# Two dense attentions: the next head's high halves on GpSimd, and the inverse sums moved out of PSUM by ScalarE

## What is computed

```python
def dense_gqa_attention(q, k, v):            # attention A: 8 heads of 64, 2 key heads
    sc = jnp.einsum('bqkgd,bskd->bkgqs', qi, k).astype(jnp.float32) * scale
    p = jax.nn.softmax(sc, axis=-1).astype(v.dtype)
    return jnp.einsum('bkgqs,bskd->bqkgd', p, v)
...
def even_mixer(...):
    oa = dense_gqa_attention(qa, ka, va) * jax.nn.silu(ga)
    ...
    # attention B: scores are a part of 64 (q_nope against keys) plus a rotary part of 32
    ob = mla_attention(q_lat, q_rope, ckv, k_rope, w_uv) * jax.nn.silu(gb)
    return jnp.concatenate([oa, ob], axis=-1) @ w_out
```

## Time and profile before

| | before |
|---|---|
| median of 3 runs | 2436.44 us (2435.43 to 2438.64) |
| the profiled execution: time, span of its core | 2435.96 us, 2434.6 us |
| TensorE busy | 2342.3 us, 96% of the span |
| VectorE, ScalarE, GpSimd busy | 1399.0, 1139.0, 893.7 us |
| shares of the chain of work that ended last | PE 80%, ACT 7%, issue 5%, DVE 4%, POOL 2% |
| attention A | about 294 to 490 us of the span |
| attention B | about 529 to 755 us of the span |

### The profile page before, as it was taken

How to read it: one execution, slowest core, us unless ns; L and a number is a source line. 1 busy time by engine, 2 the same in 40 slices (tenths; PEclk the granted TensorE clock), 3 DMA queues, 4 the chain that set the end, 5 groups by cost and what they waited for, 6 DMA issues and landing times.

```text
span 2434.6 us, 31485 instructions
## 1 busy us (share of the span) xinstructions
PE 2342.3 (96%) x12138; PEld 1936.1 (80%) x12138; DVE 1399.0 (57%) x1931; ACT 1139.0 (47%) x1778; POOL 893.7 (37%) x665
## 2 busy tenths in 40 slices
PE   5999999989999999998999999999999999999998
PEld 5778788868888888876678878788877888888887
DVE  6256499948885240129973744332576666666665
ACT  5322388868884231239962375232333333333334
POOL 1111234236662122326522212112255555565551
PEclk8999999999999999999999999999999999999999
DMA  8244300000003131100021131113111111111111
GB/s 304 75 130 139 103 6 1 1 19 1 1 1 113 35 125 44 52 9 1 10 104 44 45 116 44 29 32 121 52 44 52 52 52 52 52 52 53 57 55 70
DMA packets 152488, 143.23 MB, mean 59 GB/s; under 512 B 10358, under 2 KB 140692, under 8 KB 150420
## 3 DMA queue, kind: packets, MB, share of 16 engines
q1 hardware_dynamic: 152340, 141.22, 18.1%
HBM read 124.43 MB, written 16.78 MB: 58 GB/s over the span
## 4 chain that ended last, share of the span: by engine, by line
PE 80%; ACT 7%; issue 5%; DVE 4%; POOL 2%; DMA 0%; SPq 0%; ACTq 0%; DVEq 0%; POOLq 0%
PE ps L260 38%; PE ps L2617 15%; PE ps L2634 9%; PE ps L1103 4%; PE ps L1126 3%; PE ps L1113 3%; ACT C_PR L1773 1%; PE ps L1662 1%; POOL WSL L2534 1%; ACT B_PR L1186 1%; ACT B_PTH L1180 1%; PE ps L2593 1%; ACT C_PTH L1781 1%; PE ps L1641 1%; POOL WSR L2516 1%
## 5 line engine op out<-in xcount | busy, mean ns | idle before, releaser
L249 POOL TENSOR_TENSOR WL<-WR,WH 128x1024 fp32r<-128x1024 f32 (+1 forms) x89 | 206.3, 2318 | 805.8 <-ACT WH L244 805.6
L260 PE MATMUL ps<-HH,WH 128*128 128x512 f32 (+1 forms) x1136 | 359.8, 398 | 0.0
L260 PE MATMUL ps<-HL,WH 128*128 128x512 f32 (+1 forms) x1136 | 351.4, 391 | 0.0
L260 PE MATMUL ps<-HH,WL 128*128 128x512 f32 (+1 forms) x1136 | 351.1, 390 | 0.0
L260 PEld LDWEIGHTS ps<-HH,WL 128*128 128x128 f32 (+1 forms) x1136 | 212.7, 187 | 46.5
L260 PEld LDWEIGHTS ps<-HL,WH 128*128 128x128 f32 (+1 forms) x1136 | 212.5, 187 | 46.7
L260 PEld LDWEIGHTS ps<-HH,WH 128*128 128x128 f32 (+1 forms) x1136 | 209.1, 187 | 48.1 <-issue 6.3
L2847 DVE TENSOR_TENSOR XF<-ps,XF 128x1024 f32<-128x1024 f32 x168 | 201.6, 1220 | 32.4 <-PE ps L2634 25.8
L2617 PE MATMUL ps<-HC,WSH 128*128 128x512 f32 x640 | 197.0, 389 | 0.0
L1139 DVE TENSOR_REDUCE NM<-ps 128x1 f32<-128x1024 f32 x128 | 156.1, 1220 | 34.9 <-PE ps L1103 34.2
L2534 POOL TENSOR_TENSOR WSL<-WSR,WSH 128x512 fp32r<-128x512 f32 x100 | 131.4, 1314 | 107.5 <-ACT WSH L2528 107.5
(11 more groups left out here) (433 smaller groups left out, 5179.1 us busy)
## 6 DMA issues: line engine op xcount, KB each, us to landing
WS<-in_w_ffn_in SPq DMA_DIRECT2D x44, 512.0 KB, 4.9
MKW<-in_ada_w SPq DMA_DIRECT2D x32, 512.0 KB, 4.1
spill<-X SPq DMA_DIRECT2D x3, 4096.0 KB, 13.5
OW<-in_w_ffn_out SPq DMA_DIRECT2D x22, 512.0 KB, 3.4
WR<-in_w_in SPq DMA_DIRECT2D x20, 512.0 KB, 3.7
WR<-in_odd_w_in SPq DMA_DIRECT2D x19, 512.0 KB, 3.7
WR<-in_even_w_in SPq DMA_DIRECT2D x17, 512.0 KB, 4.9
AWK<-in_ada_w SPq DMA_DIRECT2D x8, 1024.0 KB, 9.6
```

Of the source, the lines that this page charges most:

```text
L249: pool.tensor_tensor(low[:, :, :], raw[:, :, :], high[:, :, :].bitcast(F32), ALU.subtract).then_inc(*w_low.up(t))
L260: last = pe.matmul(ps[0:w.m, 2 * s + h, :], wt[:, k, :], x[:, k, halves(h)], start=(k == 0 and n == 0), stop=(k == w.kt - 1 and n == 2))
```

## The change

Four things change, in both attentions:

1. The high halves of the next head's queries (two pieces for each of heads 1 to 7) move from ScalarE to GpSimd: `pool_query`, in GpSimd's step s % 8 = 1. ScalarE keeps the keys' and rotary highs of B, now in steps 3, 4 and 5 in place of 3, 4 and 4.
2. GpSimd's low pieces move one step later (2 to 6 in place of 1 to 5), its values from step 5 to step 7.
3. The product of the gate and the inverse sums moves from VectorE, which read the inverse sums in PSUM, to GpSimd. Since that reads a tile in SBUF, ScalarE first copies the inverse sums to a new tile `RIS` (64 x 256). There is one such tile for each attention, so ScalarE waits for GpSimd's product of the pair before.
4. GpSimd begins attention A only when the last projection of the stage before has been multiplied.

```diff
-    gated = signal("gated")
+    ri_moved = signal("ri_moved")
...
-    mixed, ri_wide, v_high, v_low, bias_low, *pool_lows = pool_made.steps("mixed", "ri_wide", "v_high", "v_low", "bias_low",
-                                                                          "q_low", "k_low", "r_low")
+    mixed, ri_wide, v_high, v_low, pool_gated, pool_q_high, *pool_lows = pool_made.steps(
+        "mixed", "ri_wide", "v_high", "v_low", "gated", "q_high", "q_low", "k_low", "r_low")
...
-    A.RID = place("A_RID", 187.5, [P, 2, HD])
+    A.RID, A.RIS = place("A_RID", 187.5, [P, 2, HD]), place("A_RIS", 43, [P, 2 * P])
...
-    B.RID = place("B_RID", 203.5, [P, 2, HD])
+    B.RID, B.RIS = place("B_RID", 203.5, [P, 2, HD]), place("B_RIS", 67, [P, 2 * P])
...
         if piece < 2:
-            if h >= 2 and piece == 0:
-                act.wait_ge(*s_done.at(g, 8 * (h - 2) + 7))
             act.activation(D.QD1[h % 2][rows(piece, HD), :], D.q(h), ACT.Copy).then_inc(*q_high.up(g, h, piece))
...
+    def pool_query(D, h, piece):
+
+        g = D.tag
+        if h >= 2 and piece == 0:
+            pool.wait_ge(*s_done.at(g, 8 * (h - 2) + 7))
+        pool.tensor_copy(D.QD1[h % 2][rows(piece, HD), :], D.q(h)).then_inc(*pool_q_high.up(g, h, piece))
+
...
-            eng.wait_ge(*q_high.at(g, h, 1))
+            eng.wait_ge(*(pool_q_high if h else q_high).at(g, h, 1))
...
-                mix = MIX[o, D.mix(h), rows(pg % 4, 2 * P)]
-                dve.wait_ge(*pv_done.at(g, pg))
-                dve.tensor_tensor(mix, ps[0:HD, 6 + pg % 2, 2 * P:4 * P], mix, ALU.mult).then_inc(*gated.up(g, pg))
...
                 act.wait_ge(*pv_done.at(g, pg))
+                if pg:
+                    act.wait_ge(*pool_gated.at(g, pg - 1))
+                act.activation(D.RIS[rows(pg // 4 % 2, HD), :], ps[0:HD, 6 + pg % 2, 2 * P:4 * P],
...
                 if pg >= 2:
                     act.wait_ge(*o2_done.at(g, pg - 2))
                 act.activation(D.OT[rows(pg // 4 % 2, HD), pg % 2, :], ps[HD:P, 6 + pg % 2, 0:2 * P],
...
             h = s // 8 + 1
             if h < 8:
-                for piece in {1: (0, 1), 3: (2,), 4: (3, 4)}.get(s % 8, ()):
-                    if piece < 2 or g == "B":
+                for piece in {3: (2,), 4: (3,), 5: (4,)}.get(s % 8, ()):
+                    if g == "B":
                         act_query(D, h, piece)
...
-                pool.wait_ge(*gated.at(g, pg))
+                pool.wait_ge(*ri_moved.at(g, pg))
+                pool_in_turn()
+                pool.tensor_tensor(mix, D.RIS[o, :], mix, ALU.mult).then_inc(*pool_gated.up(g, pg))
                 pool.wait_ge(*o2_done.at(g, pg))
                 pool_in_turn()
...
             h = s // 8 + 1
             if h < 8:
-                for piece in {1: (0,), 2: (1,), 3: (2,), 4: (3,), 5: (4,)}.get(s % 8, ()):
+                if s % 8 == 1:
+                    for piece in range(2):
+                        pool_in_turn()
+                        pool_query(D, h, piece)
+                for piece in {2: (0,), 3: (1,), 4: (2,), 5: (3,), 6: (4,)}.get(s % 8, ()):
                     if piece < 2 or g == "B":
                         pool_in_turn()
                         rest_query(pool, D, h, piece)
-                if s % 8 == 5 and D.v_first(h):
+                if s % 8 == 7 and D.v_first(h):
...
     def pool_attention_a():
         pool.wait_ge(*va_copied.at())
+        pool.wait_ge(*w_used.at(EVEN_PROJ[-1]))
```

More of the change, by code:

```diff
@@ L1190, in act_dense @@
                 act.wait_ge(*pv_done.at(g, pg))
+                if pg:
+                    act.wait_ge(*pool_gated.at(g, pg - 1))
+                act.activation(D.RIS[rows(pg // 4 % 2, HD), :], ps[0:HD, 6 + pg % 2, 2 * P:4 * P],
+                               ACT.Copy).then_inc(*ri_moved.up(g, pg))
                 if pg >= 2:
```

## The result

The changed kernel takes 2447.47 us (median of 5 runs, 2444.62 to 2449.24), the kernel before beside it 2436.44 (2434.47 to 2438.64). The ratio is 1.0041, 95% interval 1.0028 to 1.0054: slower by 11.0 us. The forecast was 2437.7, its range ended at 2446. In two later jobs the changed kernel took 2445.37 and 2445.51, which is 8.5 and 7.5 us more than the kernel before.

A forecast was written before the change was run, and what follows sets the result against it. TensorE was taken to set the pace in both attentions. A -8.6, B +8.2 (stalls 17.1 less gains 8.9) and clock +1.7 sum to +1.3 us: 2437.7 us against the median 2436.44, range 2431 to 2446.

The forecast's parts named there:

- I leave the clock at 1.00 in the stalls of 2.2 us: In B, clock loss of 1.7 us was counted only behind head 3's 5.0 us stall, none behind the shorter ones.
- the clock falls in every stall: Rival for B: five more clock falls of 1.7 us each, 2446.2 us in all; chance 0.13.
- A, step 6 to 63, -7.0: Attention A's 8.3 us excess from ScalarE's query highs goes, except 1.3 us for weight pieces: -7.0 us.
- A's start, -1.6: At A's start, ScalarE's two query copies no longer stand before the first PTH: 1.6 us gained.
- ScalarE's highs in B, -7.6: In B, moving query highs away and splitting the two rotary highs of step 4 removes all 7.6 us excess.
- The cast of 64x1024 at 1.04 us: GpSimd's new query cast, absent from the trace, takes 1.04 us by a line through smaller copies and casts.
- rival of a dearer copy: GpSimd's query cast takes 1.54 us, giving 2443.7 us, or 2.39 us, giving 2454; chance 0.10.
- The chain of 21.3 us: GpSimd's work in B from a head's first RID to its last rotary low: 19.3 us busy plus 2.0 us gaps.
- Stalls of 2.2 us each: In B, TensorE waits 2.2 us for GpSimd's last low at heads 2, 4, 5, 6 and 7: 11.0 us.
- Head 3, 5.0: In B, head 3's stall is 5.0 us, since its GpSimd chain also holds EVEN_FIRST's low and starts later.
- Head 1, 1.1: In B, head 1 waits 1.1 us: its first RID comes late and the second rotary high is made later.
- A late product in A: GpSimd's product in A, 1.2 us late, stays hidden; rival: it stops ScalarE, 8.4 us more, 2446.1 us, chance 0.07.

The follow-up runs named there:

- e1: The changed kernel run again with nothing altered: 2445.37 us, ratio 1.0032 to the kernel before.
- e11: The changed kernel again, unaltered, on the same chip as the run with shorter TensorE filler products: 2445.51 us, ratio 1.0034 to the kernel before.
- e8: Changed kernel, but B's gate product on VectorE, B's lows, values and highs not later, EVEN_FIRST's low in step 22: 2424.33 us, 0.9947 of the kernel before.
- e4: Changed kernel, but B's gate product back on VectorE and ScalarE's RIS copy gone there: 2429.09 us, 0.9968 of the kernel before.
- e6: A as changed; B as before except later steps for GpSimd's lows and values and ScalarE's second rotary high: 2432.21 us, 0.9976 of the kernel before.
- e3: Change in attention B alone, A as in the kernel before: 2455.06 us, ratio 1.0079 to the kernel before.
- e5: Changed kernel plus unused identity products on TensorE before B's waits for lows (16 a head, 34 in head 3): 2452.14 us, 1.0062 of the kernel before.
- e9: Changed kernel plus unused identity products on TensorE before B's waits for lows (8 a head, 17 in head 3): 2438.90 us, 1.0009 of the kernel before.

## Why the prediction was wrong

**The failing step** is the sentence "I leave the clock at 1.00 in the stalls of 2.2 us". It counted one fall, 1.7 us, where the profiles of after lost 5.1, 8.5 and 8.5 us to the clock in B, which made B's steps 4.2, 7.3 and 7.2 us longer. The one fall that it did count was sized too low as well: behind head 3's stall the steps were 2.4 to 2.6 us longer. The rival *the clock falls in every stall* was the right mechanism with too high a count: two to four of the six stalls of 1.8 us or more, in the three profiles of after. Its 2446.2 is nearer to the three medians (2445.4 to 2447.5) than the forecast is, and the range ended 0.2 us short of it. By the runs, the mean result is -8.1 in A, +9.1 from stalls in B (224.0 against 214.9) and +7.0 from the clock by the steps of e1 and e11: +8.0, against 8.5 and 7.5 measured there. The forecast had -8.6, +8.2 and +1.7.

The other steps:

- **A, step 6 to 63, -7.0:** measured -6.55. The weight pieces of steps 16 to 20 kept 1.7 us, not 1.3.
- **A's start, -1.6:** -1.5. **B's start, -1.3:** from 16.8 to 15.5 us, -1.3.
- **ScalarE's highs in B, -7.6:** e8 shows 191.37 us from step 6 to step 63, of 189.8 at the clean pace and 197.45 before. So 6.1 of the 7.6 came there, in a kernel whose highs stand in other steps (its start, 16.6 us, gained only 0.2). In the changed kernel the gain can't be read apart from the stalls.
- **The cast of 64x1024 at 1.04 us:** 1037 ns. The line through copies and casts held. The rival of a dearer copy is out. The estimate of 1.54 us from the price in the Trainium skill (GPSIMD Engine Reference, section 3.1) doesn't agree with this row.

```profile
L1061 POOL CAST B_QD<-QN 64x1024 fp32r<-64x1024 f32 x14 | 14.5, 1037 | 0.9
```

- **The chain of 21.3 us:** 21.0. Stalls of 2.2 us each: the steps into heads 2, 4, 5, 6 and 7 were 2.1 to 2.3 us longer than clean ones, of which 1.82 to 1.95 us are idle time of TensorE. Head 3, 5.0: 5.3, of which 1.1 came a step early, since ScalarE's `RIS` waited for GpSimd's product.

```profile
598.47 0.38 ACT L1195 ACTIVATE B_RIS<-ps 64x256 f32<-64x256 f32 x1 [1.11 <-POOL MIX L1228]
```

- **Head 1, 1.1:** the step into it was 1.84 us longer, with an idle time of 1.35 us, for the reason given. The row below starts 1.20 us late, behind ScalarE's second rotary high, and ends at 550.59; TensorE began at 550.85, 0.26 us behind it as behind every late low. (The profile puts this wait down to ScalarE's exponential.)

```profile
545.74 4.85 POOL L1079 TENSOR_TENSOR B_QRS<-QR,B_QRS 32x1024 fp32r<-32x1024 f32 x2 [1.20 <-ACT B_QRS L1054]
```

- **A late product in A:** hidden, as said. ScalarE has no wait for GpSimd there.

What the sum of parts could not give is the case of e4 and e6: a chain is as long as its busy parts only while nothing in it waits for another engine. It was true of the changed kernel, and this is why the 21.3 held.

Beside that, 11.0 us of the first job hold some 3 us of chance, since the two later jobs have 8.5 and 7.5. Their medians lie inside the range, so that the first lies outside it is in part chance. In the first profile A began 6.0 us late, as in e3's by 4.8, and e1's and e11's did not; there this is a larger part of the miss than the clock in B (4.2 against 1.7). In how many of the job's other executions A began late is not known.

## What to carry to other kernels

Before work is moved to an engine with room, count the chain that its deadline hangs on, with every wait for another engine in it: GpSimd's mean load in B before (129.65 of 216 us, 60%) showed room and said nothing about this. Where the bound engine then stalls for about 2 us again and again, price each stall with the chance of a fall of the clock behind it, here one in two at 1.6 us. Stalls of 1.66 us and less, and stalls filled with products that nobody reads, didn't pay that price here.

## What the runs showed of the hardware

Whether the clock falls behind a stall of 1.8 to 2.05 us differs between executions of the same program: in the profiles of after it fell behind head 4's in e1 and e11, and not in the first. Products of the identity were enough to hold it at 1.00 (e5, e9).

The late start of A has another cause than the change. In the stage before it, one VectorE operation ran beside a GpSimd low. Of after, VectorE and GpSimd:

```profile
243.54 1.28 DVE L529 SCALAR_TENSOR_TENSOR MKA<-MKW,CS,MKA 128x1024 f32<-128x1024 f32 x1 [2.21 <-DMA MKW<-in_ada_w]
247.40 3.38 DVE L529 SCALAR_TENSOR_TENSOR MKA<-MKW,CS,MKA 128x1024 f32<-128x1024 f32 x1 [2.57 <-DMA MKW<-in_ada_w]
```

```profile
247.35 2.34 POOL L249 TENSOR_TENSOR WL<-WR,WH 128x1024 fp32r<-128x1024 f32 x1 [8.49 <-ACT WH L244]
```

And the same VectorE operation of before, which ended ahead of GpSimd's at 247.70:

```profile
246.22 1.28 DVE L529 SCALAR_TENSOR_TENSOR MKA<-MKW,CS,MKA 128x1024 f32<-128x1024 f32 x1 [1.17 <-DMA MKW<-in_ada_w]
```

It took 3.38 us in place of 1.28, about as if it had begun when GpSimd's ended at 249.69. TensorE waited 2.95 us for it, and the clock fell to 0.50 behind that:

```profile
252.00:255.00 3.00, 3.00 (x12) 2.71 (x12) 1.09 (x3) 0.00 (x0) 0.00 (x0) 0.50 0.48 162
```

The DMA ahead of it decides which of the two starts first, so it happens in some executions. The Trainium skill (SBUF — State Buffer, section "SBUF: two separate sides") says that a VectorE operation with two inputs in SBUF and a GpSimd operation that reads SBUF exclude each other for the whole of the one that starts first; these rows agree. In e3, whose A began 4.8 us late, the same VectorE operation took 3.26 us beside the same GpSimd one; in the other eleven traces it began ahead of it and took 1.28 to 1.29 us, and A began at 293.1 to 296.3 us. No run here moved the two apart on purpose, so this cause is read from the trace and not shown by an experiment.
